# Attention by head pairs with outputs by token, two-column modulation products, and layer 1's modulation chunks spread over later stages

## What is computed

```python
for l in range(DEPTH):
    sh_m, sc_m, g_m, sh_f, sc_f, g_f = adaln(c, w_mod[l], b_mod[l])          # silu(c) @ w_mod + b_mod, split in 6
    csh_m, csc_m, cg_m, csh_f, csc_f, cg_f = adaln(c_ctx, w_mod[l], b_mod[l])
    h_lat = rmsnorm(x_lat, norm_mix[l]) * (1.0 + sc_m) + sh_m
    ...                                                                       # mixer of the layer
    x_lat = x_lat + g_m * m_lat
    h_lat = rmsnorm(x_lat, norm_ffn[l]) * (1.0 + sc_f) + sh_f
    x_lat = x_lat + g_f * moe(h_lat, router_w, router_b, moe_w1[l], moe_w3[l], moe_w2[l])

# attention of the latent tokens: band of +-128 latent keys, and all context keys
m = jnp.maximum(jnp.maximum(s_loc.max(-1, keepdims=True), s_ctx.max(-1, keepdims=True)), s_sink)
denom = p_loc.sum(-1, keepdims=True) + p_ctx.sum(-1, keepdims=True) + jnp.exp(s_sink - m)
o = (jnp.einsum('bngrqk,bnkgd->bnqgrd', p_loc / denom, vb.astype(jnp.float32))
     + jnp.einsum('bngrqc,bcgd->bnqgrd', p_ctx / denom, v_ctx.astype(jnp.float32)))
# attention of the context tokens: the same over the 256 context keys, softmax with the sink
```

## Time and profile before

| | |
|---|---|
| median of 3 runs | 1325.04 us (1325.0 to 1326.84) |
| profiled execution | 1311.33 us, its span 1309.5 us |
| busy: TensorE, weight loads, VectorE, ScalarE, GpSimd | 1105.2, 576.4, 510.6, 249.0, 224.4 us |
| granted TensorE clock, mean | 0.912 |
| chain that ended last | PE 70%, DMA 10%, DVE 10%, ACT 3% |
| read from memory | 308.41 MB, 247 GB/s over the span |

### The profile page before, as it was taken

One profiled execution on the slowest core, in us unless ns is written; L12 is line 12 of the kernel. 1 busy time (PEld: TensorE's weight loads), 2 busy tenths in 40 slices (PEclk: granted clock), 3 DMA queues, 4 the chain that ended last, 5 costly groups with the idle time before them and its releaser, 6 DMA issues.

```text
span 1309.5 us, 13521 instructions
## 1 busy us (share of the span) xinstructions
PE 1105.2 (84%) x5097; PEld 576.4 (44%) x5097; DVE 510.6 (39%) x1004; ACT 249.0 (19%) x481; POOL 224.4 (17%) x218
## 2 busy tenths in 40 slices
PE   3899978799899479999999199998868489869992
PEld 0445444443454434444455164445544355434441
DVE  0434656655501522221222678326461433322213
ACT  2222121365511400000001332111010301000001
POOL 0001031000011063333211302000001174332001
PEclk8899978899999789999999599999668789999997
DMA  9732155779161359999995832122007279999982
GB/s 354 224 106 89 66 192 193 249 260 392 63 257 67 130 197 408 409 416 415 347 400 231 330 124 69 64 102 92 1 0 321 100 270 411 413 416 417 425 333 111
DMA packets 74366, 309.79 MB, mean 237 GB/s; under 512 B 11789, under 2 KB 14013, under 8 KB 57131
## 3 DMA queue, kind: packets, MB, share of 16 engines
q1 hardware_dynamic: 63947, 292.70, 57.4%
q0 software_dynamic: 9472, 12.77, 2.8%
q10 hardware_dynamic: 864, 3.15, 0.6%
HBM read 308.41 MB, written 15.34 MB: 247 GB/s over the span
## 4 chain that ended last, share of the span: by engine, by line
PE 70%; DMA 10%; DVE 10%; ACT 3%; issue 3%; SPq 3%; POOL 1%; ACTq 0%; POOLq 0%; DVEq 0%
PE psum L1828 9%; DMA arena<-in_moe_w 9%; PE psum L1831 9%; PE psum L1196 7%; PE psum L1101 6%; PE psum L1863 5%; PE psum L551 5%; PE psum L1858 4%; PE psum L543 3%; PE psum L1209 2%; PE psum L377 2%; SPq L2023 2%; PE psum L996 2%; PE psum L1447 1%; PE psum L838 1%
## 5 line engine op out<-in xcount | busy, mean ns | idle before, releaser
L1944 POOL DMA_INDIRECT arena<-hdram,idxl x128 | 128.7, 1005 | 258.1 <-DVE arena L1903 168.7
L1918 DVE TENSOR_TENSOR arena<-arena,psum 128x512 f32<-128x512 f32 x32 | 22.0, 687 | 271.7 <-PE psum L1828 142.4
L1196 PE MATMUL psum<-arena,ring 128*128 128x512 f32 (+1 forms) x256 | 97.8, 540 | 0.0
L1828 PE MATMUL psum<-arena 128*64 128x256 f32 x736 | 82.8, 381 | 8.8 <-DMA arena<-in_moe_w 7.4
L1831 PE MATMUL psum<-ring,arena 128*128 128x512 f32 x176 | 78.9, 606 | 10.6 <-DVE arena L1903 9.8
L1828 PE MATMUL psum<-ring,arena 128*64 128x256 f32 x672 | 77.7, 389 | 11.6 <-DVE arena L1903 9.2
L1101 PE MATMUL psum<-ring,arena 128*128 128x512 f32 x192 | 82.9, 593 | 1.5 <-ACT arena L1086 1.5
L1125 POOL TENSOR_TENSOR xres<-xres,arena 128x512 f32<-128x512 f32 x12 | 15.2, 1262 | 384.2 <-DVE arena L1114 384.2
L1886 ACT ACTIVATE arena<-psum 128x512 f32<-128x512 f32 x32 | 19.1, 597 | 281.7 <-PE psum L1858 173.7
L1903 DVE STREAM_TRANSPOSE arena<-arena 128x1024 f32<-128x1024 f32 x32 | 64.9, 2029 | 18.3 <-DMA arena<-hdram,idxl 18.3
L551 PE MATMUL psum<-ring,arena 128*128 128x512 f32 (+1 forms) x192 | 69.0, 522 | 0.0
(11 more groups left out here) (369 smaller groups left out, 1572.6 us busy)
## 6 DMA issues: line engine op xcount, KB each, us to landing
ring<-in_moe_w SPq DMA_DIRECT2D x48, 2048.0 KB, 14.4
arena<-in_moe_w SPq DMA_DIRECT2D x48, 2048.0 KB, 15.5
ring<-in_w_mod SPq DMA_DIRECT2D x24, 2048.0 KB, 8.9
ring<-in_od_w_in SPq DMA_DIRECT2D x6, 2048.0 KB, 11.3
ring<-in_ev_w_in SPq DMA_DIRECT2D x3, 2048.0 KB, 9.2
arena<-ydram SPq DMA_DIRECT2D x6, 1024.0 KB, 6.9
ring<-in_ev_w_out SPq DMA_DIRECT2D x2, 2048.0 KB, 12.5
ring<-in_od_w_out SPq DMA_DIRECT2D x2, 2048.0 KB, 7.7
```

Source lines behind the costliest of these rows:

```text
L1196: mm = pe.matmul(bank(bk, tok.stop - tok.start), w[:, k, P * (b % 4):P * (b % 4) + P], hT[:, k, tok], start=k == 0, stop=k == KD - 1)
L1828: mm = pe.matmul(psum[64 * g:64 * g + 64, hbank(e, j), 0:256], xT[b][:, k, 0:64], w[:, k, 256 * g:256 * g + 256], start=k == 0, stop=k == ...
L1944: pool.indirect_dma_start(xq[e % NX][:, 256 * g:256 * g + 256], None, xrows(l), bass.IndirectOffsetOnAxis(ap=idxl[:, g, e:e + 1], axis=0), ...
```

## The change

Attention goes in 16 pairs of heads (`PAIRS`). In iteration p TensorE issues the masks and scores of pair p (its two heads in the lower and upper 64 rows of the array and in two banks of their own), the transposes of pair p-1, and the values of pair p-2 with the transposed probabilities as weights and 64 value columns moving, so that outputs stand by token. The probabilities are no longer divided: VectorE divides a tile's outputs once (`onorm`), and TensorE transposes them (`turn("tile", t)`). The sink is exponentiated once for a tile.

A chunk's columns are made by four products with the `modrow` block as weights and two columns (`streamsel`) moving, into bank 7, which the rows use too; the rows of a chunk wait until the columns of the chunk before are copied. Chunks 13 to 23 leave the attention: 13 stands between the output projection and the norm (`NORM_MOD`), 14 and 15 between the router and the MoE (`LIST_MODS`), 16 and 17 after the MoE's gate products (`COMB_MODS`), 18 to 23 in the mLSTM (`ML_MODS`). SP loads `w_out` ahead of chunks 13 to 15 and four MoE pieces ahead of chunk 15.

TensorE in a latent tile, before: two heads, with the values of four behind them. The names are tiles: `cb` constants (mask), `cf` the identity, `arena` queries, keys, probabilities and values.

The diff, cut to its core:

```diff
+    streamsel = cf[:, 618:620]
...
+    ptb = [view(16384 + 512 * i, [4, P]) for i in range(4)]
+    onorm = [view(18432 + 512 * i, [512]) for i in range(2)]
+    pbuf = [view(20480 + 512 * i, [TOK]) for i in range(4)]
...
+    NORM_MOD, LIST_MODS, COMB_MODS = MODC + 1, (MODC + 2, MODC + 3), (MODC + 4, MODC + 5)
+    ML_MODS = range(MODC + 6, 2 * MODC)
     before0 = [mod_src(*m) for m in MODS[:FIRST]]
     before0 += [cols(ev, 512, 1024), cols(ev, 1024, EV_Q), cols(ev, EV_K, 2064), cols(ev, EV_Q, EV_K), cols(ev, 0, 512)]
-    before0 += [mod_src(*m) for m in MODS[FIRST:]]
+    before0 += [mod_src(*m) for m in MODS[FIRST:NORM_MOD]]
     before0 += [cols(ev_w_out[0], 512 * i, 512 * i + 512) for i in range(2)]
-    before1 = [cols(od, OD_GATES, OD_GATES + 32)] + [cols(od, 512 * i, 512 * i + 512) for i in range(6)]
+    before0 += [mod_src(*MODS[m]) for m in (NORM_MOD, *LIST_MODS)]
+    before1 = [mod_src(*MODS[m]) for m in COMB_MODS]
+    before1 += [cols(od, OD_GATES, OD_GATES + 32)] + [cols(od, 512 * i, 512 * i + 512) for i in range(6)]
+    before1 += [mod_src(*MODS[m]) for m in ML_MODS]
     before1 += [cols(od_w_out[0], 512 * i, 512 * i + 512) for i in range(2)]
...
     def mod_pos(m):
+        if m in ML_MODS:
+            return OD0 + 7 + m - ML_MODS[0]
+        if m in COMB_MODS:
+            return OD0 - len(COMB_MODS) + m - COMB_MODS[0]
+        if m >= NORM_MOD:
+            return m + 7
         return m if m < FIRST else m + 5
     def pe_mod_rows(m):
+        if m > 0:
+            pe.wait_ge(S("mcol_done"), m)
         weights_here(mod_pos(m))
...
     def pe_mod_cols(m):
         pe.wait_ge(*pe_more("modrow_ready"))
-        if m > 0:
-            pe.wait_ge(*pe_more("mcol_done"))
         for b in range(4):
-            mm = pe.transpose(psum[:, 6, P * b:P * b + P], modrow[:, P * b:P * b + P], ident)
+            mm = pe.matmul(psum[:, 7, 2 * b:2 * b + 2], modrow[:, P * b:P * b + P], streamsel, start=True, stop=True)
         mm.then_inc(S("modcol_full"), 1)
...
         l, ch = MODS[m]
         dve.wait_ge(*dve_more("modcol_full"))
-        dve.tensor_reduce(mcol[:, l, 4 * ch:4 * ch + 4, :],
-                          bank(6).rearrange("p (b g r) -> p b r g", b=4, g=4)[:, :, 0:2, :], AX.X, ALU.add
-                          ).then_inc(S("mcol_done"), 1)
+        dve.tensor_copy(mcol[:, l, 4 * ch:4 * ch + 4, :], bank(7, 8).rearrange("p (b r) -> p b r", b=4)
+                        ).then_inc(S("mcol_done"), 1)
...
+            if ready == "res_added" and t == 3 and len(tiles) == NT:
+                act_mod(NORM_MOD)
             act.activation(htok[:, t, :], xres[:, t, :], ACT.Square, accum_out=stat[:, n:n + 1]
                            ).then_inc(S("sum_ready"), 1)
...
     ATT = [(t, h) for t in range(NT) for h in range(H)]
-    ATT_LEFT = 2 * MODC - OUT_MOD - 1
-    ATT_MOD = {(len(ATT) // ATT_LEFT) * (j + 1) - 1: OUT_MOD + 1 + j for j in range(ATT_LEFT)}
...
+        def scores(p):
+            t, j = p // 4, p % 4
+            n = nkeys(t)
+            if p >= 2:
+                pe.wait_ge(S("prob_ready"), 2 * p - 2)
+            b0 = 2 * (p % 2)
+            if lat(t):
+                for par in range(2):
+                    pe.matmul(bank(b0 + par), identb, attmask[t - 2], start=True, stop=False)
+            for par in range(2):
+                a = slice(64 * par, 64 * par + 64)
+                pe.matmul(bank(b0 + par, n), qT[a, j, P * t:P * t + P], kT2[a, j // 2, 0:n], start=not lat(t), stop=True
+                          ).then_inc(S("score_full"), 1)
+        def turn(kind, i, blocks):
+            u = turned(kind, i)
+            if u > 2:
+                pe.wait_ge(S("probT_ready"), u - 2)
+            for k, src in enumerate(blocks):
+                mm = pe.transpose(psum[:, turn_bank(kind, i), P * k:P * k + P], src, ident)
+            mm.then_inc(S("probT_full"), 1)
...
+        def values(p):
+            t = p // 4
+            if p % 4 == 0 and t >= 2:
+                pe.wait_ge(S("o_normed"), t - 1)
+            pe.wait_ge(S("probT_ready"), turned("head", 2 * p + 1))
+            nk = nkeys(t) // P
+            for i in (2 * p, 2 * p + 1):
+                h = ATT[i][1]
+                for k in range(nk):
+                    mm = pe.matmul(psum[:, obank(t), 64 * h:64 * h + 64], ptb[i % 4][:, k, :],
+                                   qkv[:, k, 640 + 64 * (h // 4):704 + 64 * (h // 4)], start=k == 0, stop=k == nk - 1)
+            mm.then_inc(S("o_full"), 1)
...
+        for p in range(PAIRS + 3):
+            if p < PAIRS:
+                scores(p)
+            if 1 <= p <= PAIRS:
+                for i in (2 * p - 2, 2 * p - 1):
+                    pe.wait_ge(S("prob_ready"), i + 1)
+                    turn("head", i, [pbuf[i % 4][:, P * k:P * k + P] for k in range(nkeys(ATT[i][0]) // P)])
+            if 2 <= p <= PAIRS + 1:
+                values(p - 2)
+            if p >= 6 and (p - 6) % 4 == 0:
+                t = (p - 6) // 4
+                pe.wait_ge(S("o_normed"), t + 1)
+                turn("tile", t, [onorm[t % 2][:, P * b:P * b + P] for b in range(4)])
...
+        for p in range(PAIRS + 3):
+            if p < PAIRS:
+                for i in (2 * p, 2 * p + 1):
+                    t, h = ATT[i]
+                    dve.wait_ge(*dve_more("score_full"))
+                    dve_step(dve.tensor_reduce(NM[:, i:i + 1], bank(i % 4, nkeys(t)), AX.X, ALU.max))
+                    dve.tensor_scalar(NM[:, i:i + 1], NM[:, i:i + 1], -0.125, NSINK[:, h:h + 1], ALU.mult, ALU.min
+                                      ).then_inc(S("max_ready"), 1)
...
+            if p >= 6 and (p - 6) % 4 == 0:
+                t = (p - 6) // 4
+                hs = slice(8 * t, 8 * t + 8)
+                dve.wait_ge(*dve_more("row_act"))
+                dve_step(dve.tensor_tensor(RDEN[:, hs], RSUM[:, hs], ESINK[:, hs], ALU.add))
+                dve_step(dve.reciprocal(RDEN[:, hs], RDEN[:, hs]))
+                dve.wait_ge(S("o_full"), 4 * t + 4)
+                if t >= 2:
+                    dve.wait_ge(S("probT_full"), turned("tile", t - 2))
+                dve.tensor_tensor(heads(onorm[t % 2]), heads(bank(obank(t))), RDEN[:, hs].unsqueeze(2).broadcast_to([P, H, 64]),
+                                  ALU.mult).then_inc(S("o_normed"), 1)
...
+        def exp(i):
...
+            act.wait_ge(S("max_ready"), i + 1)
+            if i >= 4:
+                act.wait_ge(S("probT_full"), turned("head", i - 4))
+            act.activation(pbuf[i % 4][:, 0:nkeys(t)], bank(i % 4, nkeys(t)), ACT.Exp, bias=NM[:, i:i + 1], scale=0.125,
+                           accum_out=RSUM[:, i:i + 1]).then_inc(S("prob_ready"), 1)
+        def evac(i):
+            nk = nkeys(ATT[i][0]) // P
+            act.wait_ge(S("probT_full"), turned("head", i))
+            if i >= 4:
+                act.wait_ge(S("o_full"), i // 2 - 1)
+            act.activation(ptb[i % 4][:, 0:nk, :], bank(turn_bank("head", i), P * nk).rearrange("p (k n) -> p k n", k=nk), ACT.Copy
+                           ).then_inc(S("probT_ready"), 1)
...
+        def evac_tile(t):
+            act.wait_ge(S("probT_full"), turned("tile", t))
+            act.wait_ge(S("o_normed"), t + 1)
+            act.activation(catT[:, 4:8, P * t:P * t + P], bank(turn_bank("tile", t)).rearrange("p (b n) -> p b n", b=4), ACT.Copy
+                           ).then_inc(S("o_done" if t == NT - 1 else "probT_ready"), 1)
...
-        pe.wait_ge(S("mod_done"), 6)
+        pe.wait_ge(S("mod_done"), 8 if l else 4)
+        pe.wait_ge(S("mcol_done"), 2 * MODC if l else COMB_MODS[0] if which else NORM_MOD)
...
         decays(0)
+        for m in ML_MODS[:2]:
+            pe_mod(m)
...
                     decays(1)
+                    pe.wait_ge(S("mcol_done"), 2 * MODC)
...
+            if st < 2:
+                pe_mod(ML_MODS[2 + i])
+            elif st < 3:
+                keep_busy()
...
+        for m in ML_MODS[:2]:
+            dve_mod(m)
         for i, (st, d) in enumerate(SSD_ITER):
             t = tile_of(st, d)
+            if st < 2:
+                dve_mod(ML_MODS[2 + i])
+            elif i == 4:
+                dve_mod_bias(1, 4, MODC)
+                dve_acol(1, 1)
...
+            if i == 1:
+                for m in ML_MODS:
+                    act_mod(m)
...
-    used += [("mod_full", i + 1) for i in range(FIRST, 2 * MODC)]
+    used += [("mod_full", i + 1) for i in range(FIRST, NORM_MOD)]
     used += [("out_full", 4), ("out_full", 8)]
+    used += [("mod_full", m + 1) for m in (NORM_MOD, *LIST_MODS)]
...
     used += used_in_ring(0)
+    used += [("mod_full", m + 1) for m in COMB_MODS]
     used += [("in_full", EVEN_FILLS + n) for n in (2, 6, 10, 14, 18, 20, 22)]
+    used += [("mod_full", m + 1) for m in ML_MODS]
...
-        return (S("o_done"), 2 * NT) if l == 0 else (S("cat_ready"), NT + 2)
+        return (S("o_done"), 1) if l == 0 else (S("cat_ready"), NT + 2)
...
```

(33 more changed lines are left out.)

177 lines of the change are left out of this document (64 added, 113 removed).

## The result

The change made the kernel slower: 1335.43 us (median of 20 runs, 1322.46 to 1349.26) against 1324.74 (1315.25 to 1330.07), a ratio of 1.0073 with a 95% interval of 1.0044 to 1.0102, some 10 us. The ratio is of runs made side by side and leaves out executions over 1.5% above the fastest of their kernel, here three of the 20. The forecast was 3 us less, and its range ended at 1333. The profiled execution had a span of 1333.4 us at a mean clock of 0.905.

A forecast was written before the change was run, and what follows sets the result against it. TensorE, busy 84% of the span and nearly all of the attention, was taken as the bound. Terms of -33 + 4 + 1.8 + 1.3 + 2 + 2.1 + 18.8 = -3.0 us gave 1322.0 from 1325.04, range 1312 to 1333.

The forecast's parts named there:

- Attention: Attention stage: pairs of heads, with the eleven chunks gone, take 62 us against 95.4, -33 (-37 to -26).
- rivals 1 and 5: First: latent pair's scores don't overlap, +7.5 us, chance 0.10; second: four latent heads still take 11.0, +8, chance 0.08.
- Rival 3: Attention loses its full clock; a context pair takes 3.7 us on TensorE, the whole +12; chance 0.07.
- Two-column product: Columns of the eight SSD chunks and chunk 12: dearer than four transposes by 0.44 us each, +4 in all.
- Rival 4: The chunks' two-column product is cheap, half of L838's record: -7 us, 1315 in all; chance 0.15.
- Start: Before the input projection: chunk 3's rows wait for the copy of chunk 2's columns, +1.8 us (1.0 to 2.6).
- chunks 16 and 17: After the MoE's gate products: VectorE's combination is queued behind these chunks' copies, +2.1 us (1.5 to 4).
- chunk 13: Between output projection and norm: its rows and ScalarE's copy delay the norm's last square, +1.3 us (0.5 to 2).
- Chunks 18 to 23: In the mLSTM: six chunks, 3.93 us for one by itself, delay VectorE's first addition of outputs by 18.8 us.
- rival 2: The mLSTM's chunks take 5 to 6 us more at half the clock: +3 in all, 1328; chance 0.15.
- Chunks 14 and 15: Between router and MoE: they delay the first transpose of gathered rows by 2 us, up to 6 if gathers are slow.
- The signs of being wrong: Attention over 70 us, a chunk by itself over 4.5, or the MoEs changing in length by over 3.

The follow-up runs named there:

- a4: The kernel before without chunks 13 to 23, layer 1's modulation zero: 1315.81 us, 0.9898 of the kernel before.
- a1: The changed kernel run again unaltered, for a second profile: 1339.84 us, 1.0083 of the kernel before.
- a3: The changed kernel without chunks 13 to 23, layer 1's modulation zero: 1295.06 us, 0.9725 of the kernel before.
- b2: The changed kernel with the chunks' columns again made by four transposes instead of the two-column product: 1324.96 us, 0.9982 of the kernel before.
- b3: The changed kernel with products that nothing reads filling TensorE's gaps in chunks 18 to 23: 1337.96 us, 1.0065 of the kernel before.

## Why the prediction was wrong

- **What bounds the kernel.** Read as: TensorE is busy 90.5 of 95 us, so what leaves it shortens the stage. The first half may stand, the second doesn't: a4 took the eleven chunks out, TensorE stayed busy for 87.9 of 95.0 us, and the stage kept its time at a clock of 0.68. The 36.7 us that the new attention gains came with pairs, three stages and unscaled probabilities, and without chunks; the new attention with chunks among its heads wasn't run, so how much of the gain needs their leaving isn't shown.
- **Attention**, -33: measured -36.7 at full clock and -28 to -29 where the clock falls. At full clock the steps held: 4.25 us for a latent pair (4.4), 2.06 to 2.50 for a context pair (2.2), heads side by side, so rivals 1 and 5 are out. Rival 3, the attention that loses its clock, didn't occur in the two profiles of the changed kernel, but did in four later ones, in the context tiles, at 3.80 us for a context pair (3.7 named) and 8 to 9 us in all (12 named). By the rule of the Trainium skill (TensorE: Matmul & The Clock Gate, Part 4) transposes don't count as TensorE being busy in the way that other products do. Here the same mixture of scores, transposes and 64-column products ran at a clock of 1.00 in four profiles and at about 0.50 through the context tiles of four others, so the rule alone doesn't decide this case.
- **Two-column product**, +4: +0.39 each at full clock (1.05 against 0.66), near the 0.44 taken from L838; the records start 0.112 us apart. At half clock it is 1.87 against 1.12, +0.75, which the sum hadn't. SSD and chunk 12 lost 6.5, of which 3.5 is the product. The two profiles differ here: the SSD is 2.9 us longer in a1, which the product covers, and 9.1 in after, where the mean clock over the last 75 us to its end was 0.78 against 0.86 in a1. Rival 4 is out: with two columns moving, a record costs what it does with 64. The Trainium skill's latency of 60 columns (TensorEngine Tiling (Array Packing), performance considerations) would be an estimated 25 ns and isn't what these records show; their weight loads, 192 ns busy and overlapping, are the likelier bound, which no run tests.
- **Start** (+2.0) and **chunks 16 and 17** (+2.1) were right. The stretch of **chunk 13** grew by 1.9 us for 1.3, but a3, without that chunk, gets back only 0.5 of it, so the agreement is partly chance.
- **Chunks 18 to 23**, +18.8: this is the step that failed, and it was the size of the term and not its path. It was priced from a chunk at full clock, 3.93, and the stretch grew by 24.5. At full clock the price held (20, estimated from b2). But the first three chunks, a chain of PE, ScalarE, PE, VectorE with hardly anything beside it, stood at 1.2 GHz for a part or all of their time and took 5.2 to 6.4 us each in both profiles, which by the same estimate is the other 4 us. This was rival 2, with its place and nearly its price (5 to 6), and it had a chance of 0.15 and no place in the sum. Why the clock falls there, the runs don't show; b3 and b2 kept it up from chunk 19 on, the one with fillers and the other without. A hint was in the rows: chunk 3 in the earlier trace rows took 2.82 us for rows that take 1.92 in the attention. The 0.73 of the earlier trace rows was none: before had 1.00 from 895 to 923 us, and its low clock came after.
- **Chunks 14 and 15**, +2, measured +5.5: missed in the same way in a1, where both ran at half clock (6.5 and 7.6 us, +6.9). In after the two took 5.7 and 4.2 us, and the gather behind them was late (+4.0 in all), which the forecast had named as its bound of +6 and kept out of the sum.
- **The signs of being wrong.** A chunk by itself took over 4.5 us, as named. The attention didn't pass 70. The MoE of layer 1 changed by 3.9 us in the means, over the 3 named, but it differs by 11 between the two profiles of before, so this sign says little.
- **The range.** It ended at 1333, and the time was 1335.4. On the sum of -3 the attention brings -3.7, the chunks before the MoE +3.5, those in the mLSTM +5.7, the SSD with the stretch behind it +2.5 and the three small terms +0.8, which makes +5.8. The remaining 4 us or so to the 10 measured are the mLSTM's outputs and the MoEs, which differ by as much between two profiles of one kernel; none had been given a term. Where terms missed to the slow side, a low clock was in most of them, so they shouldn't have been treated as separate chances.
